# Two transformer blocks in fp32 on one core: the FFN input product with its 512 weight columns moving, turned by VectorE and DMAs

## The reference

```
def swiglu_ffn(h, w_ffn_in, w_ffn_out):
    g, u = jnp.split(h @ w_ffn_in, 2, axis=-1)        # 1024 -> 2 x 2816
    return (jax.nn.silu(g) * u) @ w_ffn_out           # 2816 -> 1024

for layer in range(2):
    u = rms_norm_2(h, norm_mix_pre[layer])
    m = shortconv_fox_mixer(u, ...) if layer % 2 == 0 else conformer_conv_module(u, ...)
    h = h + rms_norm_2(m, norm_mix_post[layer])
    f = swiglu_ffn(rms_norm_2(h, norm_ffn_pre[layer]), w_ffn_in[layer], w_ffn_out[layer])
    h = h + rms_norm_2(f, norm_ffn_post[layer])
```

## Time and profile before

| | us |
|---|---|
| median of 3 runs | 1102.3 |
| lowest and highest run | 1102.25, 1103.65 |
| profiled execution | 1101.02 |
| its span, first to last instruction | 1099.7 |
| TensorE busy | 1078.9 |
| VectorE busy | 741.5 |
| ScalarE busy | 596.2 |

### The profile page before, as it was taken

The page is one execution under the profiler, slowest core; times in us unless marked ns, Lnnn a source line. Parts: engine busy times, 40 slices in busy tenths (PEclk is TensorE's granted clock), DMA queues, the critical chain, the costliest instruction groups (busy, mean ns, idle before and its releaser), DMA issues.

```text
span 1099.7 us, 19172 instructions
## 1 busy us (share of the span) xinstructions
PE 1078.9 (98%) x7752; PEld 985.2 (90%) x7752; DVE 741.5 (67%) x1322; ACT 596.2 (54%) x1082; POOL 50.7 (5%) x64
## 2 busy tenths in 40 slices
PE   8999999999999999999999999999999999999998
PEld 7998888898799998889887999998899879999886
DVE  3578777996688887776567666674565566666643
ACT  4465575666776665345356645553383467554442
POOL 0260000110000001010000000000000000000000
PEclk9999999999999999999999999999999999999999
DMA  8966953652365554656424565545544144555441
GB/s 356 391 224 228 374 203 114 249 223 104 116 210 179 183 183 165 252 229 222 153 106 153 176 244 192 191 135 209 201 159 156 42 153 173 192 192 185 160 154 39
DMA packets 30765, 208.14 MB, mean 189 GB/s; under 512 B 3539, under 2 KB 4051, under 8 KB 6997
## 3 DMA queue, kind: packets, MB, share of 16 engines
q1 hardware_dynamic: 30676, 206.91, 51.7%
HBM read 205.85 MB, written 1.05 MB: 188 GB/s over the span
## 4 chain that ended last, share of the span: by engine, by line
PE 90%; DVE 4%; ACT 4%; issue 2%; DMA 1%; POOL 0%; ACTq 0%; DVEq 0%
PE ps L414 46%; PE ps L1821 20%; PE ps L1591 4%; PE ps L648 3%; PE ps L432 3%; DVE wlo L373 1%; PE ps L1427 1%; PE ps L2487 1%; PE ps L2519 1%; ACT whi L365 1%; PE ps L893 1%; PE ps L1521 1%; PE ps L1948 1%; PE ps L1425 1%; PE ps L657 1%
## 5 line engine op out<-in xcount | busy, mean ns | idle before, releaser
L373 DVE TENSOR_TENSOR wlo<-raw,whi 128x1024 fp32r<-128x1024 f32 (+2 forms) x328 | 373.6, 1181 | 210.7 <-ACT whi L365 210.4
L365 ACT ACTIVATE whi<-raw 128x1024 fp32r<-128x1024 f32 (+2 forms) x328 | 315.6, 1011 | 155.9 <-PE ps L1821 100.8
L414 PE MATMUL ps<-H_h,whi 128*128 128x256 f32 x1376 | 389.0, 283 | 0.1
L414 PE MATMUL ps<-H_h,wlo 128*128 128x256 f32 x1376 | 384.2, 279 | 0.0
L414 PE MATMUL ps<-H_l,whi 128*128 128x256 f32 x1376 | 384.1, 279 | 0.0
L414 PEld LDWEIGHTS ps<-H_h,whi 128*128 128x128 f32 x1376 | 258.3, 188 | 1.8 <-issue 1.6
L414 PEld LDWEIGHTS ps<-H_h,wlo 128*128 128x128 f32 x1376 | 258.9, 188 | 0.0
L414 PEld LDWEIGHTS ps<-H_l,whi 128*128 128x128 f32 x1376 | 258.6, 188 | 0.2
L1821 PE MATMUL ps<-whi,gl_h 128*128 128x512 f32 x264 | 105.3, 399 | 0.6 <-DVE wlo L373 0.6
L1821 PE MATMUL ps<-whi,gl_l 128*128 128x512 f32 x264 | 104.2, 395 | 0.0
L1821 PE MATMUL ps<-wlo,gl_h 128*128 128x512 f32 x264 | 103.8, 393 | 0.0
(11 more groups left out here) (474 smaller groups left out, 1652.1 us busy)
## 6 DMA issues: line engine op xcount, KB each, us to landing
raw<-f SPq DMA_DIRECT2D x44, 1024.0 KB, 4.8
raw<-win SPq DMA_DIRECT2D x27, 1024.0 KB, 6.6
raw<-ada SPq DMA_DIRECT2D x24, 1024.0 KB, 5.4
raw<-up SPq DMA_DIRECT2D x22, 1024.0 KB, 4.8
raw<-g SPq DMA_DIRECT2D x20, 1024.0 KB, 4.8
raw<-pw SPq DMA_DIRECT2D x12, 1024.0 KB, 4.8
raw<-down SPq DMA_DIRECT2D x10, 1024.0 KB, 6.1
raw<-wa SPq DMA_DIRECT2D x4, 1024.0 KB, 9.6
```

Source lines behind the costliest of these rows:

```text
L365: act.activation(whi[j % NS][:, a:b], raw_of(key)[:, a:b], ACT.Copy).then_inc(w_hi.hit(key, half), 1)
L373: dve.tensor_tensor(wlo[j % NS][:, a:b], raw_of(key)[:, a:b], whi[j % NS][:, a:b].bitcast(F32), ALU.subtract).then_inc(w_lo.hit(key, half), 1)
L414: ins_ = pe.matmul(bank[:, m * 256:(m + 1) * 256], wt[a][:, kt * w + col + m * 128:kt * w + col + m * 128 + 128], act[b][:, k0 + kt, :], s ...
```

## The change

1. *Form of the input product.* "f0" and "f1" are units of (4, 512). Five chunks of 512 gate and 512 value features have four units each (gate, contraction halves 0 and 1; value, the same), a sixth chunk of 256 and 256 has two. Tokens are the stationary operand, 512 weight columns move, the result has its tokens on the partitions.
2. *What follows.* The root is now a number for each partition, so silu takes it as its scale and VectorE's one product as its scalar, and `rn_pe` and the per-unit multiply are gone. VectorE turns 32x32 blocks into `blk` (one instruction for each token half), and SP moves the blocks to their partitions with 16 DMAs for each chunk into `fmaj`, standing in its list before the load of unit 4c+11 (29 for the last chunk). ScalarE and VectorE then split `fmaj` into `gl` over 1024 columns at a time. The rows of the output weights are permuted on the host to fit the order of features that comes out.
3. *Start.* Four tiles of X's first 128 tokens are turned before the last three matmuls of the output product in front, and the first unit runs over these tokens while the others are being normalised; the rest is turned in quarters between. `xroots_act` stands after all parts of H and ahead of the split of the third unit.
4. *End.* The hi and lo of the last two chunks of `gl` stand between the splits of the output product's first three units.
5. *Places.* The split buffers, `gl`, `yc` and a new pair `Hw` start at 384 modulo 512 (before, the split buffers 32 bytes apart modulo 128); `H` lies over `Hw`, 64 bytes below it in its high part and 32 above in its low part. `Hw` is used by the FFN and by "pw2".
6. *Splits in attention* are put half by half into two turns.

```diff
-    "f0": [(8, 256)] * 22, "g0": WIDER,
+    "f0": [(4, 512)] * 22, "g0": WIDER,
-    "f1": [(8, 256)] * 22, "g1": WIDER,
+    "f1": [(4, 512)] * 22, "g1": WIDER,
...
+    LIKE = 384
+    def sb(name, shape, dt=F32, like=False):
...
+        at = -(-(place[0] - LIKE) // 512) * 512 + LIKE if like else place[0]
...
+            to.append(sb(f"{name}{i}", [128, 2048], F32R, True))
+    Hw_l = sb("Hw_l", [128, 8, 256], F32R, True)
+    H_l = nc.alloc_sbuf_tensor_at("H_l", [128, 8, 256], F32R, offset=place[0] - 8192 + 32)
...
+    Hw_h = sb("Hw_h", [128, 8, 256], F32R, True)
+    H_h = nc.alloc_sbuf_tensor_at("H_h", [128, 8, 256], F32R, offset=place[0] - 8192 - 64)
...
-                if n == gate_turns(i)[0]:
-                    next_hi(act, ("win", 7 + i))
+                if n - gate_turns(i)[0] in (0, 1):
+                    next_hi(act, ("win", 7 + i), (n - gate_turns(i)[0],))
...
-            if n == WO_AT[1]:
-                next_hi(act, ("wo", 0))
+            if n in WO_AT[0:2]:
+                next_hi(act, ("wo", 0), (n - WO_AT[0],))
...
+                    if late and (cb, g, t, kt) == (1, per - 1, 1, nk - 1):
+                        late(pe)
...
+            if front:
+                front((0, 1))
             msq_act(act, name, 1, 1)
+            if front:
+                front((2, 3))
             root_act(act, "m_" + name, 1)
...
+            if front and t:
+                front((0, 1))
             mg_dve(dve, name, post, 1, t, given(1))
+            if front and t:
+                front((2, 3))
...
+    def half_turn(pe, gen, name, t, half):
+        if half == 0:
+            for j in range(2):
+                x, old = M.take(n_lo(gen, t, 6 + j))
...
+        pe.wait_ge(*x_dve(name, t, half))
+        for k in range(4 * half, 4 * half + 4):
+            pe.transpose(where["xt", gen, t, k % 2][:, k // 2 * 128:k // 2 * 128 + 128], X[:, t, k * 128:(k + 1) * 128],
+                         cc("ident")).then_inc(xt.hit(gen, t, k), 1)
...
+    def ffn_pe(pe, n, gen, name):
...
+                    if c == 0 and part == "gate" and half == 0:
+                        for t in range(2):
+                            for kt in range(4):
...
+                                ins_ = chunk_step(pe, key, where[n, c, part, t], 0, kt, t, kt == 0, False)
+                                if t == 0 and kt == 3:
+                                    half_turn(pe, gen, name, 1, 0)
+                                    spin_7(pe, (gen, 1), 1)
+                                if t == 1 and kt == 0:
+                                    half_turn(pe, gen, name, 0, 1)
+                        ins_.then_inc(unit.hit(*key), 1)
+                        half_turn(pe, gen, name, 1, 1)
...
+    def chunk_mul(dve, n, gen, c):
...
+            dve.scalar_tensor_tensor(out=x(c, t), in0=value_out(n, c, t), scalar=sv(gen, 6 + t), in1=x(c, t), op0=ALU.mult,
+                                     op1=ALU.mult).then_inc(u_mul.hit(n, c, t), 1)
+        for t in range(2):
...
+            dve.transpose(blk[:, t, 0:width(c)], x(c, t)).then_inc(blk_set.hit(n, c, t), 1)
+
+    def chunk_moves(sp, n, c):
+        w = width(c) // 4
+        sp.wait_ge(*blk_set(n, c, 1))
+        for r in range(4):
+            for q_ in range(4):
+                sp.dma_start(moved(c)[32 * q_:32 * q_ + 32, :, r * w:r * w + w],
+                             blk[32 * r:32 * r + 32, :, q_ * w:q_ * w + w]).then_inc(fmaj_in[c % 2].hit(n, c, r, q_), 16)
...
+    def ffn_act(act, n, gen, gain, name):
+        split_hi(act, (n, 1), (0,))
+        for k in range(4):
+            part_hi(act, gen, gain, 1, k)
+        for k in range(4, 8):
+            for t in range(2):
+                part_hi(act, gen, gain, t, k)
+            if k == 5:
+                split_hi(act, (n, 1), (1,))
+        xroots_act(act, name, gen)
+        for u in range(1, NF):
+            next_hi(act, (n, u))
+            if u % 4 == 2 and u < 20:
+                chunk_silu(act, n, gen, u // 4)
+            if u % 4 == 2 and u > 2:
+                chunk_hi(act, n, u // 4 - 1)
...
+        chunk_silu(act, n, gen, CHUNKS - 1)
...
+    def rest_hi(act, n):
+        return lambda i: chunk_hi(act, n, 4 + i) if i < 2 else None
...
+    MOVES_AT = {AT[n, 0] + (29 if c == CHUNKS - 1 else 4 * c + 11): (n, c) for n in ("f0", "f1") for c in range(CHUNKS)}
```

More of the change, by code:

```diff
@@ L1786, in ahead_pe, with wide_pe @@
             ins_.then_inc(unit.hit(*key), 1)
-    def wide_pe(pe, name, act, ready, bias=False, between=None, ahead=0, ks=range(NF)):
+    def wide_pe(pe, name, act, ready, bias=False, between=None, ahead=0, ks=range(NF), late=None):
         per = len(UNITS[name]) // 2
@@ L1868, in added, with out_act @@
         return lambda t, cb: x_dve(name, t, cb)
-    def out_act(act, name, post, gen, scale):
+    def out_act(act, name, post, gen, scale, between=None, front=None):
         act.preload_act_table_set("natural_log_exp_and_others")
@@ L1876, in out_act @@
                 next_hi(act, (name, i))
+            if between:
+                between(i)
             if i == per:
@@ L1919, in x_dve_add, with out_dve @@
             dve.tensor_tensor(x, x, m, ALU.add).then_inc(x_dve.hit(name, t, cb), 1)
-    def out_dve(dve, name, post, gen, scale, given, between=None):
+    def out_dve(dve, name, post, gen, scale, given, between=None, front=None):
         per = len(UNITS[name]) // 2
@@ new lines, in front_turn, with tile_of, part_hi @@
+    def front_turn(gen, name):
+        return lambda pe: half_turn(pe, gen, name, 0, 0)
+    def tile_of(gen, t, k):
+        return where["xt", gen, t, k % 2][:, k // 2 * 128:k // 2 * 128 + 128]
+    def part_hi(act, gen, gain, t, k):
+        act.wait_ge(*xt(gen, t, k // 4 * 4 + 3))
+        if k >= 2:
+            act.wait_ge(*n_lo(gen, t, k - 2))
+        act.activation(Hw[0][:, k, t * 128:t * 128 + 128], tile_of(gen, t, k), ACT.Copy, scale=gain(k)).then_inc(
+            n_hi.hit(gen, t, k), 1)
@@ new lines, in part_lo, with spin_7 @@
+    def part_lo(dve, gen, gain, t, k):
+        sl = slice(t * 128, t * 128 + 128)
+        dve.wait_ge(*n_hi(gen, t, k))
+        dve.scalar_tensor_tensor(out=Hw[1][:, k, sl], in0=tile_of(gen, t, k), scalar=gain(k),
+                                 in1=Hw[0][:, k, sl].bitcast(F32), op0=ALU.mult, op1=ALU.subtract).then_inc(
+            n_lo.hit(gen, t, k), 1)
+    def spin_7(pe, key, n):
+        if bank7[0]:
+            pe.wait_ge(*bank7[0])
+        for _ in range(n):
+            ins_ = pe.matmul(banks[7][:, 0:256], cc("ident"), con[:, 0:256], start=True, stop=True)
+        ins_.then_inc(spun.hit(key), 1)
+        bank7[0] = spun(key)
@@ new lines, in chunk_bank, with chunk_step @@
+    def chunk_bank(pe, n, c, part, t, ring, reader):
+        x, old = ring.take(reader)
+        if old:
+            pe.wait_ge(*old)
+        where[n, c, part, t] = x
+    def chunk_step(pe, key, x, k0, kt, t, first, last):
+        j = SAT[key]
+        wt = (whi[j % NS], wlo[j % NS])
+        for i, (a, h) in enumerate(PR):
+            ins_ = pe.matmul(x[:], Hw[h][:, k0 + kt, t * 128:t * 128 + 128], wt[a][:, kt * 512:kt * 512 + 512],
+                             start=first and i == 0, stop=last and i == 2)
+        return ins_
@@ new lines, in gate_out, with value_out, width, act_out @@
+    def gate_out(n, c, t):
+        return where[n, c, "both", t][:, 0:256] if c == CHUNKS - 1 else where[n, c, "gate", t][:]
+    def value_out(n, c, t):
+        return where[n, c, "both", t][:, 256:512] if c == CHUNKS - 1 else where[n, c, "value", t][:]
+    def width(c):
+        return 256 if c == CHUNKS - 1 else 512
+    def act_out(c, t):
+        return uw[t][:].rearrange("p m t -> p (m t)")[:, 0:width(c)]
+    def moved(c):
+        return fmaj_end if c == CHUNKS - 1 else fmaj[c % 2]
+    def chunk_silu(act, n, gen, c):
+        for t in range(2):
+            if t == 0:
+                act.wait_ge(*unit(n, 21 if c == CHUNKS - 1 else 4 * c + 1))
+            act.wait_ge(*rs(gen, t))
+            if c:
+                act.wait_ge(*blk_set(n, c - 1, t))
+            act.activation(act_out(c, t), gate_out(n, c, t), ACT.Silu, scale=sv(gen, 6 + t)).then_inc(u_silu.hit(n, c, t), 1)
@@ new lines, in ffn_dve @@
+    def ffn_dve(dve, n, gen, gain):
+        for k in range(4):
+            part_lo(dve, gen, gain, 1, k)
+        split_lo(dve, (n, 1), (0,))
+        for k in range(4, 8):
+            for t in range(2):
+                part_lo(dve, gen, gain, t, k)
+            if k == 5:
+                split_lo(dve, (n, 1), (1,))
+        for u in range(1, NF):
+            next_lo(dve, (n, u))
+            if u % 4 == 0:
+                chunk_mul(dve, n, gen, u // 4 - 1)
+            if u % 4 == 3 and u > 3:
+                chunk_lo(dve, n, u // 4 - 1)
+            if n == "f0" and u in (18, 20):
+                tap_parts_dve(dve, (u - 18) // 2)
+        chunk_mul(dve, n, gen, CHUNKS - 1)
```

212 lines of the change are left out of this document (118 added, 94 removed).

## The result

The changed kernel takes 1125.5 us (median of 4 runs, 1122.75 to 1127.6) and the kernel before, on the same chip, 1102.7 us (4 runs, 1102.25 to 1103.65): a ratio of 1.0205, 95% interval 1.0182 to 1.0228. It is slower by 23 us, far above the forecast range. Its profiled execution took 1127.6 us with a span of 1126.3 us, 26.6 us over the span of before.

A forecast was written before the change was run, and what follows sets the result against it. TensorE, busy for 98% of the span, was taken to bound the kernel. Two FFNs at -1.9 + 3.1 + 0.6 gave +3.6 us, attention -3.0, places -1.0: -0.4 in all, 1101.9 us as a median, range 1096 to 1106.5 us.

The forecast's parts named there:

- Input to output product: Seam between FFN products: one 0.5 us wait goes, a fourth-output-unit wait comes; +0.6 us a FFN, bounds -1.0 and +1.6.
- rival 2: The clock falls in the new hole before the third FFN unit: +1.7 us a FFN, 1105.3 us; chance 17%.
- The start of the FFN: Up to the third unit: earlier first matmul, but its split waits behind the roots; +3.1 us, bounds +1.9 to +4.4.
- E+19.3: Third unit's weights ready 19.3 us after E, where the output stream in front ends; before, that unit began at E+16.26.
- Steady chunks at zero: Silu, product, transposes, 16 DMAs and splits of each chunk are covered: zero; issues of 0.8 us would cost about 2.
- Pace: Input product's units 3 to 22 at 5.55 us each: 111.0 instead of 112.92 us, -1.9 us a FFN.
- the bound called better than any seen: Lower bound for an input product unit, 5.45 us, giving -3.9 us a FFN.
- its own sign of being wrong: The prediction called itself wrong if input product units ran well under 5.5 us.
- the argument from TensorE's two read ports: From the Trainium skill: a port for each operand, so places would not count and units stay at 5.56 us.
- Places for the 256-column units: Some 57 units of 256 columns with H at new offsets: -0.6 us, between -1.1 and +1.1.
- Attention: Halved splits shorten TensorE's waits behind whole splits: -3.0 us, bounds -4.0 and +0.5.
- no case above 1108 us: Slowest case: places give nothing or the wrong way, or DMAs late; 1108 us at worst, 1105 nearer; chance 14%.

The follow-up runs named there:

- e11: e6 with the splits of the last two chunks put back ahead of the second and third output units' splits: 1107.4 us.
- e6: e1 plus seam edits: last chunk's transposes get their own buffer, its moves go one load earlier, last two chunks' splits follow the second and fourth output units: 1093.1 us.
- e3: The kernel before with only the new places in SBUF: 1107.3 us.
- e13: e6 with the SBUF places of the kernel before: 1097.7 us.
- e2: The changed kernel without its 192 block moves, transposes writing straight to `fmaj`, so that part of the turn is not computed: 1099.2 us.
- e9: e6 with the block moves issued by GpSimd: 1103.5 us.
- e10: e2 with e1's edit, so the block moves are left out and that part of the turn is not computed: 1090.9 us.
- e12: e1 with only the splits of the last two chunks moved behind the second and fourth output units: 1105.5 us.
- e1: The changed kernel with ScalarE's split for the third FFN unit ahead of the roots of X: 1113.1 us.
- e5: The changed kernel with the third unit's hi split ahead of the roots and all 192 block moves issued by GpSimd: 1118.1 us.
- e8: The changed kernel with e6's three seam edits but without e1's edit, so the roots stay ahead of the third unit's split: 1102.4 us.
- e4: The kernel before with only the attention splits put half by half into two turns: 1101.1 us.

## Why the prediction was wrong, point by point

- **Input to output product: the step that failed.** It said +0.6 a FFN, at most +1.6, and measured +7.9 and +9.4. Three things went wrong in it. (1) SP's pitch: 0.64 us a move where two 1 MB weight loads had shown 0.47; a load from another memory, of another shape, was the nearest row and no bound. Chunk 4's last move lands at 1057.2, 18.3 us behind the end of its last unit (two units of 5.45 before 1049.82, so 1038.9); the forecast had 15.4. (2) The wait of the last chunk's transposes for chunk 4's moves was not listed. VectorE's program stands with it ahead of the second output unit's split; the whole first hole comes from this, and e11, which takes that wait away, loses just that hole. (3) For the fourth output unit the mechanism was named and its size was off: 2.5 us in the first FFN and 3.8 in the second (start to start, less a matmul) for 1.8, because the second batch of moves is itself late behind the load for which SP waits. The two output products are 9.9 and 11.3 us longer than e6's 59.7. The holes are 4.8 + 2.5 and 4.3 + 3.8 us of that, and the lower clock behind them 2.4 and 3.0.
- **The clock (rival 2).** Named, with 17%, at 1.7 us a FFN for one hole. In the changed kernel the lower clock stands behind every hole of 3.4 us and over: for 6.8 us behind both holes ahead of a third unit and behind the first FFN's first hole at the seam, for 3.4 us behind each of the second FFN's two; and for 6.8 us each in front of attention and at the layer norm. That is 40.8 us in mid-run against 3.4. A matmul of 512 columns takes 0.43 us there for 0.23. Behind the holes 15, 14, 12, 7 and 8 matmuls start in these stretches, which makes some 11 us (an estimate), and in front of attention some 3 more; the holes themselves are 6.4 us at the starts and 15.4 at the seams. So the clock is the smaller part of the loss. It doubles a hole only at the starts (3.2 + 3.0); at the seams it adds a third to a half. Part of it goes with the run: the four runs of the changed kernel had a mean granted clock of 0.981, 0.982, 0.988 and 0.990 and spans of 1126.3, 1125.6, 1122.8 and 1121.4 us, and the profiled one has the lowest, while the profiled run of the kernel before has the highest that its runs show (0.998; they go down to 0.992).
- **The start of the FFN.** Right in place and size: +3.1 forecast, +2.3 in the rows; third unit at E+19.3 forecast and at E+18.57; the hole of 3.3 us measured 3.45 less a matmul, 3.2. What was missing is its consequence above.
- **Steady chunks at zero.** Nearly right: ScalarE did wait for moves (5.0 us at 1035.41), and TensorE for 0.5 to 1.0 us in two chunks of the first FFN and one of the second. "About 2 us in each" with pitches of 0.8 was not reached at 0.64.
- **Pace.** Forecast 231 ns, measured 227 to 228: at the bound called better than any seen (5.45 us a unit), and so at the edge of its own sign of being wrong. 20 units take 480 x 0.2272 = 109.1 us; the 112.83 measured contain 2.8 us of lower clock and a wait of 1.0. That the places set it was right (e3, e13); the argument from TensorE's two read ports, by which they would not count, has 5 ns against it.
- **Places for the 256-column units.** Forecast -0.6; they cost 2.2 to 2.5 us a stage of 22 units wherever 120.2 ns sets in, which was in e2, e3, e6, e9, e10 and e12, and not in the changed kernel, e1, e5, e8 and e11, with the same places. What decides it stays open.
- **Attention.** -3.0 forecast, -2.6 up to the start of "wo" (-2.7 in e4), right. The first 608 us are 1.7 us longer in the changed kernel all the same: its stage of 96 matmuls at the lower clock from 161.3 takes 13.35 us for 11.27, and the 32 matmuls before it 4.60 for 3.48.

The chances had 30% for slower, and no case above 1108 us. The first hole of each seam had no term, the second was too small, and the lower clock, which in this kernel follows most holes, stood apart as a rival and for the starts alone.

## What to carry to other kernels

A wait put in front of an in-order engine's queue is to be priced by what stands behind it, on every engine that reaches it, also for the buffer that is written again; here the same slow moves cost over 20 us in one order (e1 against e10) and 2 in another (e6 against e10). In a kernel in which TensorE is hardly ever idle, price each new hole of over 3 us with the lower clock behind it: here that added from a third of the hole's own length to as much again. A new kind of DMA should be costed from a wide range, as its pitch was a third off the nearest row here, and its landing depended on who issued it.

## What the runs showed of the hardware

- The pace of a 512-column matmul depends on where its operands lie in SBUF: 232 to 234 ns with the kernel before's places, 227 to 228 with all at 384 modulo 512 (e13 against e6, e3 against before). Which property of the places counts is not shown. A 256-column product has two paces, 117.7 and 120.2 ns a matmul, with the same places in different kernels (e6 and e11).
- A 32 KB move within SBUF over 32 partitions costs SP 0.64 us to issue and lands after 1.9; from GpSimd 0.53 and 3.5. The Trainium skill (DMA: Bandwidth & Descriptors, "Anatomy of one DMA — SWDGE (gpsimd) path") gives some 2 us of fixed cost for a DMA issued by GpSimd and puts it mostly on the completion. GpSimd's 3.5 does not agree; SP's 1.9, another path, is near it.
- Behind holes of 3.4 to 5.2 us between matmul starts TensorE ran at 1.2 GHz for 3.4 or 6.8 us, in every case but one (e8, 3.48 us before the second FFN's third unit). At 3.0 to 3.1 us it went either way: two holes of e5 were followed by 3.4 us of it, one of e9 was not. Holes of 2.7 us in the changed kernel and 2.6 in e1 were not followed by it.
